# Expert stage: h moved to memory and back, and a ring of ten result buffers in place of two

## The reference, cut to what matters

```
u = RMSNorm(h)
expert_id, weights = top-1 of 4 groups, then top-2 of 8 experts in it      # 32 experts
hid = silu(u @ w_gate[e]) * (u @ w_up[e])       # 2048 -> 256
out = hid @ w_down[e]                           # 256 -> 2048
y = h + weights_hi * out_hi + weights_lo * out_lo
```

## Time and profile before

| | us |
|---|---|
| median of 3 runs | 3697.1 (3693.54 to 3697.33) |
| the profiled execution, its own time | 3702.95 |
| span of its profile | 3701.1 |
| PE busy with matmuls, share of the span | 2911.6, 79% |
| DVE, ACT, POOL busy | 567.2, 221.8, 68.3 |
| first token gather of the expert stage | starts at 2918.75 |
| last store of a tile's result | issued at 3658.33 |

### The profile page before, as it was taken

How to read it: one execution, slowest core, us unless ns; L and a number is a source line. 1 busy time by engine, 2 the same in 40 slices (tenths; PEclk the granted TensorE clock), 3 DMA queues, 4 the chain that set the end, 5 groups by cost and what they waited for, 6 DMA issues and landing times. The chain is left out here.

```text
span 3701.1 us, 32496 instructions
## 1 busy us (share of the span) xinstructions
PE 2911.6 (79%) x12555; PEld 1947.8 (53%) x12555; DVE 567.2 (15%) x1284; ACT 221.8 (6%) x537; POOL 68.3 (2%) x74
## 2 busy tenths in 40 slices
PE   8994999956658879888888797999998554465664
PEld 7882777735446747657567465777743221122221
DVE  0001001543321120111111201000000300011112
ACT  0001001201210000000000000000000000000000
POOL 0000000000000000000000000000000100010001
PEclk9997999965556576665765767999999776787887
DMA  5425333230025444444453442333332698866664
GB/s 188 136 91 190 119 125 102 91 151 0 1 95 195 148 159 146 143 158 131 162 168 134 153 159 80 125 125 118 120 114 92 276 421 350 353 253 258 248 278 174
DMA packets 153669, 604.16 MB, mean 163 GB/s; under 512 B 23081, under 2 KB 55986, under 8 KB 115954
## 3 DMA queue, kind: packets, MB, share of 16 engines
q1 hardware_dynamic: 137074, 554.87, 41.5%
q0 software_dynamic: 9200, 31.89, 2.4%
q10 hardware_dynamic: 7312, 16.25, 1.2%
HBM read 698.46 MB, written 34.36 MB: 198 GB/s over the span
## 5 line engine op out<-in xcount | busy, mean ns | idle before, releaser
L1061 PE MATMUL bank<-zt,arena 128*128 x2688 | 564.9, 365 | 17.0 <-DMA arena<-in_fox_k 15.8
L1061 PEld LDWEIGHTS bank<-zt,arena 128*128 128x128 f32 x2688 | 562.2, 326 | 20.1 <-issue 18.7
L1081 PE MATMUL bank<-arena,ut 128*64 128x512 f32 (+1 forms) x832 | 346.2, 584 | 52.6 <-ACT ut L1104 52.6
L423 PE MATMUL bank<-ut,wring 128*128 128x320 f32 x1408 | 382.6, 433 | 0.0
L423 PEld LDWEIGHTS bank<-ut,wring 128*128 128x128 f32 x1408 | 267.3, 191 | 110.4 <-issue 1.3
L1251 PE MATMUL bank<-ut,wring 128*128 128x320 f32 x1024 | 280.2, 434 | 10.1 <-DMA ut<-u_kept 10.1
L1081 PEld LDWEIGHTS bank<-arena,ut 128*64 128x64 f32 x832 | 130.5, 160 | 257.8 <-issue 188.7
L1251 PEld LDWEIGHTS bank<-ut,wring 128*128 128x128 f32 x1024 | 195.6, 191 | 91.8 <-DMA ut<-u_kept 10.2
L1763 PE MATMUL bank<-cst,arena 128*128 128x128 f32 x208 | 42.8, 372 | 153.4 <-DVE arena L1864 105.2
L1784 PE MATMUL bank<-wgu,arena 128*32 128x512 f32 x1024 | 134.2, 657 | 26.2 <-DMA wgu<-in_w_gu 25.4
L1784 PE MATMUL bank<-wgu_x,arena 128*32 128x512 f32 x640 | 96.8, 759 | 70.9 <-DMA wgu_x<-in_w_gu,w_at 70.9
(11 more groups left out here) (346 smaller groups left out, 2004.3 us busy)
## 6 DMA issues: line engine op xcount, KB each, us to landing
wgu<-in_w_gu SPq DMA_DIRECT2D x128, 1024.0 KB, 14.1
wring<-in_w_merge SPq DMA_DIRECT2D x64, 1024.0 KB, 4.9
arena<-in_fox_k SPq DMA_DIRECT2D x128, 512.0 KB, 3.7
arena<-in_fox_v SPq DMA_DIRECT2D x128, 512.0 KB, 3.4
wdn<-in_w_dn SPq DMA_DIRECT2D x32, 2048.0 KB, 20.2
wring<-in_w_proj SPq DMA_DIRECT2D x44, 1024.0 KB, 4.9
arena<-in_cmp_kv SPq DMA_DIRECT2D x64, 256.0 KB, 3.0
zt<-in_cmp_kv SPq DMA_DIRECT2D x64, 256.0 KB, 3.0
```

The source lines that it names most:

```text
L423: last = nc.tensor.matmul(m.bank[:, 2 + s % 2, 0:T], m.wring[:, s, k * P:(k + 1) * P], m.ut[:, k, :], start=(k == 0), stop=(k == KD - 1))
L1061: last = nc.tensor.matmul(m.bank[:, SBANK[x] + bk, col:col + w], slot[:, j * P:(j + 1) * P], q, start=True, stop=True)
L1081: last = nc.tensor.matmul(m.bank[0:C, bk, 0:width], ss[:, buf, pg, :], slot[:, j * width:(j + 1) * width], start=(pg == 0), stop=False)
```

## The change

- `h_kept` is a new tensor in memory. In the route stage ACT stores h to it, 2.6 MB, right after its square root and before the stores of `u_tok`. The wait at the end of ACT's list counts this store too.
- The result buffers `yt` become ten slices of 512 columns, which take exactly the place of h (columns 5120 to 10239). `yt1` goes. There are ten semaphores `y_free`. The copy of tile j waits for the store of tile j-10.
- When PE has done the last `first`, SP loads h into a free part of the space of the base weights (`hb`). The last additions and the store of the output use it there. DVE waits for that load before it adds.
- POOL waits for all ten semaphores before it gathers the results.

`ORDER`, the weight buffers, all gathers and all arithmetic stay as they are.

```diff
+NY = 10
...
-        self.yt1 = sb("yt1", P, 512)
...
-        self.yt = [m.flat[:, 2 * DM + 512:2 * DM + 1024], self.yt1[:, :]]
+        self.yt = [m.flat[:, KD * T + 512 * s:KD * T + 512 * s + 512] for s in range(NY)]
...
             nc.scalar.activation(rs, rs, ACT.Sqrt, bias=m.eps[:, :], scale=1.0 / DM).then_inc(rs_ready, 1)
+            act.dma_start(a["h_kept"], m.flat[:, KD * T:2 * KD * T]).then_inc(un_out, 16)
             act.wait_ge(un_ready, 2)
...
-            act.wait_ge(un_out, 64)
+            act.wait_ge(un_out, 80)
...
+        hb = back[:, 5 * DM:5 * DM + KD * T]
+        hb01 = hb[:, 0:2 * DM].rearrange("p (b n) -> p b n", b=2)
+        h_in = sem("h_in")
...
+            sp.wait_ge(gu_done, NTILE)
+            sp.dma_start(hb, a["h_kept"]).then_inc(h_in, 16)
             sp.wait_ge(add_step, 6)
-            sp.dma_start(a["y_tok"], m.flat[:, KD * T:2 * KD * T]).then_inc(m.stores, 16)
+            sp.dma_start(a["y_tok"], hb).then_inc(m.stores, 16)
...
-            for s in range(2):
-                pool.wait_ge(y_free[s], 16 * (NTILE // 2))
+            for s in range(NY):
+                pool.wait_ge(y_free[s], 16 * ((NTILE - s + NY - 1) // NY))
...
                     act.dma_start(a["y_slot"][TILE_OF[j] * TW:(TILE_OF[j] + 1) * TW, :].rearrange(
-                        "t (j n) -> j t n", j=4), e.yt[j % 2]).then_inc(y_free[j % 2], 16)
+                        "t (j n) -> j t n", j=4), e.yt[j % NY]).then_inc(y_free[j % NY], 16)
...
-                    if j >= 2:
-                        dve.wait_ge(y_free[j % 2], 16 * (j // 2))
-                    nc.vector.tensor_copy(e.yt[j % 2], m.bank[:, 6 + j % 2, :]).then_inc(y_ready, 1)
+                    if j >= NY:
+                        dve.wait_ge(y_free[j % NY], 16 * (j // NY))
+                    nc.vector.tensor_copy(e.yt[j % NY], m.bank[:, 6 + j % 2, :]).then_inc(y_ready, 1)
+            dve.wait_ge(h_in, 16)
             dve.wait_ge(back_in, 96)
...
-                    nc.vector.scalar_tensor_tensor(out=m.h01[:, b, :], in0=got[b][j], scalar=w[:, b:b + 1],
-                                                   in1=m.h01[:, b, :], op0=ALU.mult, op1=ALU.add).then_inc(add_step, 1)
-                hv = m.h2[:, :, :].rearrange("p q n -> p (q n)")
+                    nc.vector.scalar_tensor_tensor(out=hb01[:, b, :], in0=got[b][j], scalar=w[:, b:b + 1],
+                                                   in1=hb01[:, b, :], op0=ALU.mult, op1=ALU.add).then_inc(add_step, 1)
+                hv = hb[:, 2 * DM:2 * DM + 1024]
```

More of the change, by code:

```diff
@@ L1680, in experts_stage @@
         dn_done, y_ready, y_free, y_tail, back_in = (
-            sem("dn_done"), sem("y_ready"), [sem("y_free0"), sem("y_free1")], sem("y_tail"), sem("back_in"))
+            sem("dn_done"), sem("y_ready"), [sem(f"y_free{s}") for s in range(NY)], sem("y_tail"), sem("back_in"))
         add_step, gu_free = sem("add_step"), sem("gu_free")
@@ L2055 @@
     a["u_tok"] = nc.dram_tensor("u_tok", (T, DM), FP32, kind="Internal").ap()
+    a["h_kept"] = nc.dram_tensor("h_kept", (P, KD * T), FP32, kind="Internal").ap()
     a["y_slot"] = nc.dram_tensor("y_slot", (SLOTS_E, DM), FP32, kind="Internal").ap()
```

## The result

| | before | after |
|---|---|---|
| median, us | 3697.22 (3693.54 to 3707.29, 4 runs) | 3642.42 (3639.99 to 3646.99, 4 runs) |
| profiled execution: own time, span | 3702.95, 3701.1 | 3646.99, 3645.2 |
| ratio to before | | 0.9849, 95% interval 0.9827 to 0.9871 |

The kernel got 54.8 us faster, not 80.1, and 3642.4 lies just above the range, whose end was 3640. The spans of the two profiled executions differ by 55.9 us, and that is the sum to be explained.

What follows compares the result with a forecast made beforehand. PE was held by waits for result stores at turns and boundaries, elsewhere by the gather loop; 15.2 + 19.6 + 40.5 + 7.1 - 1.5 - 0.8 = 80.1 us gave 3617.0, with 8 in 10 between 3598 and 3640.

Steps and rivals of the forecast that it cites:

- step 1, tiles alone: Lone tiles at the start, to 3130 us: PE asks for weights during two turns, winning back 15.2 us of transfer time.
- The lower bound of 7.6: Lone tiles at the start: half the 15.2 us gain, if PE's requests still leave gaps.
- Step 2, first pairs: From `second` of base tile 12 to `first` of more tile 3: gain 19.6 us, between 9.9 and 25.1.
- Step 3, boundaries: Three boundaries among later pairs: `first` starts when its gather lands, gain 3 x 13.5 = 40.5 us; the more group's turn stays.
- the rival of gathers that bunch up: Fuller DMA engines make gathers land in 18.11 us, not 10.5: smaller gain, about 3655 us, chance 0.13.
- Step 4, last pairs: From the gather for more tile 17 on: `wdn_x` issued earlier, gain 7.1 us, between 5 and 13.
- nothing behind it has slack: Behind more tile 17's earlier `wdn_x` in the last pairs: the 7.1 us gain was taken to hold to the end.
- h to memory: Store of h at the route stage's end, 6.1 us of transfer hidden while the router computes slots: cost 0.
- h back: Load of h after the last `first`, sharing engines with the last `wdn_x` gather: cost 1.5 us, between 0 and 6.1.
- its own range: Whole kernel, main forecast at chance 0.72: 3606 to 3634 us, with landings at boundaries 8 to 14 us.
- The signs: Profile after: buffer waits near zero, DMA share 1.0 near 3090, more tile 7 some 48 us earlier, final gathers 80.
- if the first pairs were short of weights: First pairs: one of two conditions named under which the prediction would be wrong; no size given.

Runs made afterwards that it cites:

- the first experiment: The changed kernel with each result store cut into four by quarter of the columns, so it runs on 16 DMA engines: 3593.34 us, ratio 0.9716.

## Why the prediction was wrong

**The step that failed: step 1, tiles alone.** It took the share of 0.62 in 3090 to 3130 as "15.2 us of transfer time was lost", laid the loss on PE's two turns and gave it back in full. A mean share over 16 engines says nothing about the fullest of them: in 14 of those 40 us it stood at 0.25, four engines at work. The runs show what sets this time in its place: the engines that carry the stores, and not the waits in the turns. Up to `second` of base tile 12 it is 255.5 to 258.0 us with the stores on four engines, with 2, 3, 4 or 10 buffers, and 240.4 to 241.0 with the stores on 16, with 2, 3 or 10. So the change gained -2.3 us here, and a longer ring gains nothing here on 16 engines either. That the first experiment gained 14.7 us at this place, near the 15.2, is chance: it removed a cost that step 1 had not seen. The lower bound of 7.6 had the wrong doubt in it: it asked whether PE would request in time, and not whether four engines could deliver.

**Step 2, first pairs: right** (21.2 for 19.6). The gather for more tile 2 landed in 14.73 us where 16 was taken, the one for more tile 3 in 10.30 for 10.5.

**Step 3, boundaries: right where it was worked out, too large for what stays.** The three gave 12.6, 13.1 and 14.0, together 39.7 for 40.5. But 5.9 us went again between and behind them: the step right behind each of the three took 3.1, 1.8 and 0.8 us longer than before. The chain of waits after shows part of it at the first:

```profile
3327.85 4.11 DMA arena<-u_tok,tok_at
...
3338.00 12.49 DMA wgu_x<-in_w_gu,w_at
```

The more group's token gather took 2.3 us behind this boundary before and takes 4.1 now; behind the other two it is 2.7 for 2.2. The gather behind it landed in 12.49 us, over the median of 10.6. So that the more group's turn "stays" was wrong by 1.8 us at the first and by 0.4 at the others. This is the rival of gathers that bunch up, in small: it does happen, for some of the gathers, and is not what took the 24 us.

**Step 4, last pairs: its sum right, its last words wrong.** `wdn_x` of more tile 17 was issued 63.7 us earlier than before, 9.0 more than more tile 16's 54.7 (7.1 predicted). That "nothing behind it has slack" failed: the next gather took 10.60 us where it had taken 5.3:

```profile
3557.26 10.60 DMA wgu_x<-in_w_gu,w_at
...
3578.18 4.39 DMA wgu_x<-in_w_gu,w_at
```

2.4 us stayed. Pulled forward, this gather ran beside other traffic: the DMA share is 0.67 at 257 GB/s in its 11 us, and was 0.28 at 91 GB/s in the 5 us before. That the traffic is the cause is likely, and no run separates it.

**h to memory: right.** The first token gather starts at 2918.75 in both kernels, and the idle stretch from 2900 took the traffic (0.31 where it was 0.01). That they agree to the hundredth is chance, since the other profiles have this start from 2913.1 to 2916.0; but those with h's store (2913.1 to 2916.0) and those without (2913.2 and 2913.4) begin alike.

**h back: mis-sized, or at least not settled.** The chain from the last `first` to the final gathers grew by 0.9 us where 2.3 was allowed for. Alone, with two buffers, it grew by 3.8 and the whole of h's trip cost 6.7; with the stores on 16 engines the chain is 22.7 us with the trip, and without it 19.9 with two buffers and 18.5 with three. So these say 3 to 4 us where the changed kernel says 0.9, and the runs leave open which holds for the changed kernel; if the 6.7 does, the ring itself gave 61.5 (54.8 + 6.7).

**The range and the landings.** With step 2 at its lower end and landings of 14 us at the boundaries the sum is 59.9 us, which is 3637 and not the 3634 that the prediction gives for its own range. It also took 18.11 us for the longest landing of a gather of gate and up weights; the trace before has one of 20.3. Neither changes the outcome, as 3642.4 lies above both.

**Rule weighed.** The fit of the Trainium skill that the prediction cites ("DMA: Bandwidth & Descriptors", "Anatomy of one DMA") gave an estimate of 2.6 us for a store. It is a fit for DMAs of the GpSimd path, and this store is on ACT's queue. Beside the store of the tail, 7.04 us in the profile after, stands the tail store of the first experiment with 16 engines: 1.75 us for the last of its four parts, and 3.0 us from the issue of the first part (3550.68) to the landing of the last:

```profile
3601.36 7.04 DMA y_slot<-arena
```

```profile
3551.97 1.75 DMA y_slot<-arena
```

So the disagreement that the prediction noted, two to seven times, was a hint: even without company a store took 6.27 us. Four engines at a sixteenth of 427 GB/s each need 2.5 us for its bytes, sixteen 0.6; what the rest of the 6.27 is, the runs don't show. I read the disagreement as load and did not ask how many engines carry a store.

**The signs.** DVE's and PE's waits, the share of 1.0 around 3090 and the 2918.75 came; more tile 7 (33.5 for 48) and the final gathers (56.2 for 80) did not. The share of 1.0 was a poor sign, as it came without the gain it stood for. Of the two things named that would make the prediction wrong, "if the first pairs were short of weights" did happen, PE's 23.85 us, but it does not explain the miss: PE stood 20.45 us at the same place in the first experiment, which is 49.1 us faster.

## What to carry to other kernels

A mean DMA share that stands at a plain fraction (0.25, 0.125) while someone waits for a transfer need not be idle time to be won back: a few engines may be full, and the first question is which DMA uses only them. Count a queue's packets against its DMAs, and look at the slowest dimension of both sides, before buffers are added to hide a slow store; here rewriting the store was worth 83 us, ten buffers 55, and with the store rewritten one more buffer in spare space did what ten had done. A gain that comes out as predicted should be looked for, at the same place, in a run without the change: 14.7 us for 15.2 looked like a proof here and had another cause. And a gather pulled forward is priced with the traffic it then meets, not with the quiet in which it used to run.

## What the runs showed of the hardware that was not expected

- The number of engines that carry a store sets the time of other queues' transfers too: with 52 stores of 256 KB on 4, 16 or 2 engines the kernel takes 3642.4, 3593.3 or 3758.2 us, with the same bytes.
- An engine that issues DMAs can be held while it issues them. With the stores on two engines ACT was held up to 40 us and 392.7 us in all ahead of its next copy (20.1 in the changed kernel), and PE stood 147.0 us for it. What holds it, the runs don't show.
- A store on four engines took 18.12 us beside weight traffic and 6.27 without, on 16 engines 6.77 beside it. The Trainium skill, "DMA: Bandwidth & Descriptors", section "Queues, rings and completion order", says that an engine takes turns between its queues packet by packet. The trace agrees with a store that is slow by company; that its small packets each wait for a large one of the weights would fit, but no run here changed the packets' size.
- Sixteen engines kept 429 GB/s over 40 us in the first experiment, with stores among the weights.
- A gather of gate and up weights that moves nothing, since its indices lie past the end, is still slow to land: the median of the 20 gathers, most of them empty, is 10.5 us, and 8.9 to 9.2 with the stores on 16 engines.
